# Dividing 544 tokens at 256 instead of at 272, with both parts of a result in one run of PSUM

## The chip, the cores and the metric

The kernel is one program on one core of one Trainium2 chip. TensorE multiplies, VectorE (DVE) and ScalarE (ACT) take the results out of PSUM, GpSimd (POOL) adds squares, and SyncE (SP) issues most transfers. The metric is the device time of one execution in microseconds.

## The reference

One decoder layer in float32 works on 512 prompt tokens and 8 x 4 sample tokens, 544 in all, each of 1024 values:

```
x = x + 0.5 * rmsnorm(swiglu(rmsnorm(x, f1_pre), f1_in, f1_out), f1_post)     # w_in 1024 x 5632, w_out 2816 x 1024
h = rmsnorm(x, mix_pre)
gq, gk, gv, gg, la, sq, sk, sv = project(h, w_in, gate_w, gate_b)             # 1024 x 3088
m = merge(gla(gq, gk, gv, la), gg, stick_breaking(sq, sk, sv, cache), w_out)  # 1024 x 1024
x = x + rmsnorm(m, mix_post)
x = x + 0.5 * rmsnorm(swiglu(rmsnorm(x, f2_pre), f2_in, f2_out), f2_post)
x = x + rmsnorm(sigmoid(rmsnorm(x, ple_pre) @ ple_w_gate) * (p @ ple_w_up), ple_post)
```

A dense product multiplies a weight matrix with the activations of all 544 tokens. The outputs are x and the new keys, values and states.

## The kernel before

Activations lie transposed: 128 features on the partitions, tokens along the row. `x`, `y`, `e`, `proj`, `rstd` and `glr` are declared with the tokens as two halves of `HALF = T // 2 = 272`, and `flat` (L106) joins the two to 544; the operands of the dense products, `a_hi`, `a_lo`, `h_hi` and `h_lo`, have plain rows of 544. Rows follow each other without gaps, so a row starts 2176 bytes after the one before.

A dense product is made of three products of type fp32r: each weight tile and each activation tile is split into a high part and the rest, and high x high, high x low and low x high are added up in PSUM. `dense` (L434) runs over the 128-row tiles `k` of the contraction, over one or two result tiles `c`, over the three combinations, and innermost over the two halves of the tokens. So each `mm` of L444 has a stationary operand of 128 x 128, which is loaded anew for each half, and a moving operand of 128 x 272. A PSUM bank holds 512 fp32 numbers per partition; half 0 of a result lies in columns 0 to 271 of one bank, half 1 in columns 0 to 271 of the next. Four banks are a quad; the steps of a stage use the two quads by turns. There are 8304 such products: 3168 in each of the two FFNs (`up0` 12 steps, `down0` 8, `up1` 10, `down1` 8), 1200 in the input projection `in` (its last step has 16 stationary columns), 384 in `out` and 384 in `gate`.

Other products over all tokens have the same division: the sums of squares (L455, `sum_norm`), the sums of the head norms (L807), the embedding (L490) and the gate logits (L639).

The readers of PSUM take both halves in one instruction, by `banks` (L280): a pattern of 2 x 272 numbers with a step of 512, or 4 x 272 for two result tiles. They are on DVE the gate and up parts of an FFN step (L1223, L1224), the second half of a down product (L1239), the projections (L1276, L1281, L1285), the forget gate (L1366), the first embedding (L1564) and the output gate (L1576); on ACT they are the norms (L859, L1097) and copies (L911, L1106, L1131).

The order of the work is written out by hand. Each engine runs its own program and waits on semaphores: TensorE waits for a split weight (`split_lo`), for a free quad (`psum_free`) and at the start of a stage for each input tile (`a_lo_ready`, `h_lo_ready`); the readers wait for `psum_full`, the last product of a step. SP loads a weight (two transfers of 512 KB) when the split of the weight two before it is done.

Of the kernel before, what the change touches and what calls it, by code (L numbers as in the profile page):

```python
# [20 lines left out]
P = 128  # L21
# [6 lines left out]
HALF = T // 2  # L28
# [77 lines left out]
def flat(ap):  # L106

    return ap.rearrange("p a t -> p (a t)")


def build(nc, a, o):
# [13 lines left out]
    with ctx:  # L125
# [8 lines left out]

        x = sb("x", [P, KD, 2, HALF])
        y = sb("y", [P, KD, 2, HALF])
# [22 lines left out]
        rstd = sb("rstd", [P, 2, 2, HALF])  # L159
        work = sb("work", [P, 2, T])  # L160
        glr = sb("glr", [GLA_RANK, 2, HALF])
# [18 lines left out]
        with nc.sbuf_tensor("proj", [P, 24, 2, HALF], F32) as proj:  # L180
            pass
        with nc.sbuf_tensor("rows", [P, 5, D_MODEL], F32) as rows, nc.sbuf_tensor("e", [P, KD, 2, HALF], F32) as e:
            pass
# [15 lines left out]
        gs = scratch(work_flat, 0, [P, 2, HALF])  # L199
        us = scratch(work_flat, T, [P, 2, HALF])  # L200
        dead = proj[:, SV:SV + 8].rearrange("p k a t -> p (k a t)")
# [7 lines left out]
        y_flat = y[:].rearrange("p k a t -> p (k a t)")  # L209
# [8 lines left out]
        q_pad = [rstd[:, n].rearrange("p a t -> p (a t)") for n in range(2)]  # L218
# [23 lines left out]
        la_raw, la_soft = rstd[:, 0].rearrange("p a t -> p (a t)"), sum_sq[:]  # L242
# [37 lines left out]
        def banks(quad, first, n):  # L280
            return PS[:, 4 * quad + first:4 * quad + first + n, 0:HALF]
# [139 lines left out]
        def _(pe):  # L421
# [58 lines left out]
            def embed(s_):  # L480

                t, slot = embed_ticket(s_), W0["embed"] % 2
                weights(W0["embed"])
                open_t(t)
                for k in range(2):
                    for c in range(2):
                        for n, (wt, act) in enumerate(((w_hi, p_hi), (w_hi, p_lo), (w_lo, p_hi))):
                            for half in range(2):
                                col = k * D_MODEL + (2 * s_ + c) * P
                                last = mm(PS[:, 4 * (t % 2) + 2 * c + half, 0:HALF], wt[:, slot, col:col + P],  # L490
                                          act[:, k, half * HALF:(half + 1) * HALF],
                                          start=(k == 0 and n == 0), stop=(k == 1 and n == 2))
                last.then_inc(sig["psum_full"], 1)
# [142 lines left out]
            def gate_logits(p):  # L636

                for half in range(2):
                    last = mm(PS[:, 6 + half, 0:HALF], gate_w[:, p * P:(p + 1) * P], glr[:, half], start=True, stop=True)  # L639
                last.then_inc(sig["la_full"], 1)  # L640
# [161 lines left out]
            for i in range(KD):  # L802
                t = T0["merge"] + i
                open_t(t)
                pe.wait_ge(sig["m_sq"], i + 1)
                for half in range(2):
                    last = mm(PS[:, 4 * (t % 2) + half, 0:HALF], (ones if i < 4 else ones64)[:],  # L807
                              sq[:, i % 2, half * HALF:(half + 1) * HALF], start=True, stop=True)
                last.then_inc(sig["psum_full"], 1)
# [32 lines left out]
        def _(act):  # L842
# [12 lines left out]
            def norm(j):  # L855

                t, r = sum_ticket[j], rstd[:, j % 2]
                full(act, t)
                fn(r, banks(t % 2, 0, 2), ACT.Ln, bias=eps[:], scale=1.0 / D_MODEL).then_inc(psum_free[t % 2], 1)  # L859
                act.wait_ge(psum_free[t % 2], t // 2 + 1)  # L860
                fn(r, r, ACT.Exp, scale=-0.5).then_inc(sig["rstd_ready"], 1)
# [47 lines left out]
            def down0(st, t, quad, use):  # L909
                full(act, t)  # L910
                fn(y[:, bass.ds(st.n, 1)].rearrange("p k a t -> p (k a) t"), banks(quad, 0, 2),  # L911
                   ACT.Copy).then_inc(psum_free[quad], 1)

            def down1(j):
                def body(st, t, quad, use):

                    act.wait_ge(psum_free[quad], use + 1)
                    n = 8 * j + st.n
                    act.wait_ge(sig["sq_used"], n - 1)
                    fn(sq[:, st.parity(0), :], y[:, bass.ds(st.n, 1)].rearrange("p k a t -> p (k a t)"),  # L920
                       ACT.Square).then_inc(sig["sq_ready"], 1)
                return body
# [167 lines left out]
            for i in range(KD):  # L1090
                if i + 1 < KD:
                    head_square(i + 1)
                t, r = T0["merge"] + i, rstd[:, i % 2]
                full(act, t)
                if i >= 2:
                    act.wait_ge(sig["m_ready"], i - 1)
                fn(r, banks(t % 2, 0, 2), ACT.Ln, bias=eps[:],  # L1097
                   scale=1.0 / (GLA_DV if i < 4 else SB_DH)).then_inc(psum_free[t % 2], 1)
                act.wait_ge(psum_free[t % 2], t // 2 + 1)
                fn(r, r, ACT.Exp, scale=-0.5).then_inc(sig["m_norm"], 1)  # L1100
                act.wait_ge(sig["m_ready"], i + 1)
                fn(a_hi[:, i, :], decay[i % 2], ACT.Copy).then_inc(sig["a_hi_ready"], 1)

            def out_body(st, t, quad, use):
                full(act, t)
                fn(y[:, 2 * st.c:2 * st.c + 2].rearrange("p k a t -> p (k a) t"), banks(quad, 0, 4),  # L1106
# [21 lines left out]
            def e_tiles(n):  # L1128
                t = embed_ticket(n)
                full(act, t)  # L1130
                fn(e[:, 2 * n:2 * n + 2].rearrange("p k a t -> p (k a) t"), banks(t % 2, 0, 4),  # L1131
# [30 lines left out]
        def _(dve):  # L1162
# [52 lines left out]
            def up(name, j):  # L1215
                base = up_base[name]

                def body(st, t, quad, use):
# [4 lines left out]
                    v.tensor_tensor(gs, banks(quad, 0, 2), r, ALU.mult).then_inc(sig["g_ready"], 1)  # L1223
                    v.tensor_tensor(us, banks(quad, 2, 2), r, ALU.mult).then_inc(psum_free[quad], 1)  # L1224
# [11 lines left out]
            def down1(st, t, quad, use):  # L1236
                full(dve, t)
                yt = y[:, bass.ds(st.n, 1)].rearrange("p k a t -> p (k a) t")
                v.tensor_tensor(yt, banks(quad, 0, 2), yt, ALU.add).then_inc(psum_free[quad], 1)  # L1239
# [33 lines left out]
            def project(st, t, quad, use):  # L1273
                full(dve, t)
                if st.c == 12:
                    v.tensor_tensor(glr[:], PS[0:GLA_RANK, 4 * quad:4 * quad + 2, 0:HALF], rstd[0:GLA_RANK, 0],  # L1276
                                    ALU.mult).then_inc(psum_free[quad], 1)
                elif st.c == 0:

                    for c in range(2):  # L1280
                        ins = v.scalar_tensor_tensor(proj[:, GQ + c], banks(quad, 2 * c, 2), GLA_DK ** -0.5,  # L1281
                                                     rstd[:, 0], ALU.mult, ALU.mult)
# [80 lines left out]
            for p in range(2):  # L1363
                dve.wait_ge(sig["la_full"], p + 1)
                dve.wait_ge(sig["cum_ready"], p)
                v.tensor_scalar(rstd[:, 0], PS[:, 6:8, 0:HALF], vec[:, 64 + p:65 + p], None,  # L1366
# [13 lines left out]
            for hh in range(2):  # L1380
                r = slice(64 * hh, 64 * hh + 64)
                dst = y[r, 4:8].rearrange("p k a t -> p k (a t)")[:, :, SEQ:T].rearrange("p k (b t) -> p k b t", t=DEC_SEQ)
# [116 lines left out]
            def sample_outs(p):  # L1499
                dve.wait_ge(sig["on_full"], p + 1)  # L1500
                src = PS[:, 4, 0:64].rearrange("p (b h t) -> p h b t", h=2, t=DEC_SEQ)
                dst = y[:, 2 * p:2 * p + 2].rearrange("p k a t -> p k (a t)")[:, :, SEQ:T].rearrange(
# [61 lines left out]
            v.tensor_copy(e[:, 0:2].rearrange("p k a t -> p (k a) t"), banks(t % 2, 0, 4)).then_inc(psum_free[t % 2], 1)  # L1564
            boundary(2, 5, "f2_post", "ple_pre", 4)
            for n in range(4):
# [8 lines left out]
                for c in range(2):  # L1575
                    ins = v.tensor_tensor(work[:, c, :].rearrange("p (a t) -> p a t", a=2), banks(quad, 2 * c, 2),  # L1576
# [9 lines left out]
        def _(pool):  # L1586
# [92 lines left out]
            for hh in range(2):  # L1679
                r = slice(64 * hh, 64 * hh + 64)  # L1680
                q_ = proj[r, SQ:SQ + 4].rearrange("p k a t -> p k (a t)")[:, :, SEQ:T].rearrange(
# [89 lines left out]
```

## Time and profile before

| | |
|---|---|
| time, median of 3 executions | 1465.97 us (1462.32 to 1467.61) |
| profiled execution, first to last instruction | 1466.9 us |
| TensorE (PE) busy | 1342.8 us, 92%, 9669 products |
| DVE busy | 607.3 us, 41% |
| ACT busy | 429.2 us, 29% |
| POOL busy | 147.9 us, 10% |
| DMA | 110.00 MB, mean 75 GB/s |

The profiled execution has no time of its own beside its span of 1466.9 us, which lies between the median and the highest of the three. Engines: PE is TensorE's products, PEld its weight loads, which run beside them. "L444" is line 444 of the kernel. A product's mean ns in the profile is its latency, from its first column in to its last out; products overlap, so the pace has to be read from the starts of neighbours. The clock column is the granted share of TensorE's 2.4 GHz. Times in the timeline are us from the start of the span, and one row of it may hold several instructions ("x2").

### The profile page before, as it was taken

What the parts mean: (1) busy time and instruction counts of PE and PEld (TensorE: products, weight loads), DVE (VectorE), ACT (ScalarE), POOL (GpSimd) and SP (SyncE); (2) the same over time, 40 slices, a digit from 0 to 9 for tenths busy, and PEclk for the clock granted to TensorE, in tenths of its full rate; (3) what the DMA queues carried; (4) which work ended last, traced back from release to release, by engine and by line L of the source; (5) the groups of instructions that cost most, each with busy time, mean ns of one, the idle gap of its engine ahead of it and who ended that gap; (6) DMA issues with size and microseconds to landing.
All of it is one profiled execution on the core that took longest, in us unless ns stands there. A gap on an engine that the chain in (4) does not pass through costs nothing.

```text
span 1466.9 us, 22802 instructions
## 1 busy us (share of the span) xinstructions
PE 1342.8 (92%) x9669; PEld 1271.9 (87%) x9669; DVE 607.3 (41%) x650; ACT 429.2 (29%) x497; POOL 147.9 (10%) x159
## 2 busy tenths in 40 slices
PE   3999999999995999989988878779999999999895
PEld 2999999999995999867777647779999999999894
DVE  5244422344337233234427743364443134433843
ACT  3222222222324111245411134432222222222543
POOL 3200000000013000010003301230000000001311
PEclk9999999999998999979956868889999999999997
DMA  6133233332231222311310002312322333223101
GB/s 174 32 86 86 75 87 99 99 92 73 72 107 44 86 86 59 134 43 43 130 44 17 15 17 73 87 30 72 93 78 75 99 99 86 75 73 102 67 29 61
DMA packets 168149, 110.00 MB, mean 75 GB/s; under 512 B 5147, under 2 KB 160878, under 8 KB 168094
## 3 DMA queue, kind: packets, MB, share of 16 engines
q1 hardware_dynamic: 166450, 104.15, 24.2%
q0 software_dynamic: 1472, 5.01, 1.1%
q8 instruction: 41, 0.67, 0.2%
q14 instruction: 14, 0.11, 0.0%
q10 hardware_dynamic: 172, 0.05, 0.0%
HBM read 103.57 MB, written 5.64 MB: 74 GB/s over the span
## 4 chain that ended last, share of the span: by engine, by line
PE 84%; DVE 9%; ACT 3%; issue 2%; SPq 1%; POOL 1%; DMA 0%; POOLq 0%; ACTq 0%; DVEq 0%
PE PS L444 70%; DVE work L1185 2%; PE PS L666 2%; DVE a_lo L1176 2%; PE PS L714 1%; DVE x L1197 1%; PE PS L577 1%; PE PS L606 1%; PE PS L772 1%; PE PS L455 1%; PE PS L775 1%; PE PS L603 1%; PE PS L586 1%; PE PS L555 1%; DMA raw<-in_f_in 0%
## 5 line engine op out<-in xcount | busy, mean ns | idle before, releaser
L444 PE MATMUL PS<-a_hi,w_hi 128*128 128x272 f32 (+1 forms) x2064 | 435.8, 293 | 39.6 <-DVE a_lo L1176 23.5
L444 PE MATMUL PS<-a_lo,w_hi 128*128 128x272 f32 (+1 forms) x2064 | 431.4, 291 | 0.0
L444 PE MATMUL PS<-a_hi,w_lo 128*128 128x272 f32 (+1 forms) x2064 | 430.6, 291 | 0.0
L444 PEld LDWEIGHTS PS<-a_hi,w_hi 128*128 128x128 f32 (+1 forms) x2064 | 327.5, 191 | 46.3 <-issue 21.9
L444 PEld LDWEIGHTS PS<-a_lo,w_hi 128*128 128x128 f32 (+1 forms) x2064 | 328.3, 191 | 0.5
L444 PEld LDWEIGHTS PS<-a_hi,w_lo 128*128 128x128 f32 (+1 forms) x2064 | 326.0, 191 | 0.5
L1170 DVE TENSOR_TENSOR w_lo<-raw,w_hi 128x2048 fp32r<-128x2048 f32 (+2 forms) x97 | 202.1, 2083 | 230.5 <-ACT w_hi L853 230.5
L853 ACT ACTIVATE w_hi<-raw 128x2048 fp32r<-128x2048 f32 (+2 forms) x97 | 166.0, 1712 | 116.2 <-PE PS L444 114.6
L444 PE MATMUL PS<-h_hi,w_hi 128*128 128x272 f32 x704 | 145.3, 287 | 0.0
L444 PE MATMUL PS<-h_hi,w_lo 128*128 128x272 f32 x704 | 144.8, 288 | 0.0
L444 PE MATMUL PS<-h_lo,w_hi 128*128 128x272 f32 x704 | 144.6, 287 | 0.0
L903 ACT ACTIVATE work<-work 128x544 f32<-128x544 f32 x44 | 29.0, 660 | 346.4 <-DVE work L1223 346.4
L1223 DVE TENSOR_TENSOR work<-PS,rstd 128x544 f32<-128x544 f32 x44 | 31.9, 725 | 237.2 <-PE PS L444 219.5
L444 PEld LDWEIGHTS PS<-h_lo,w_hi 128*128 128x128 f32 x704 | 110.0, 188 | 0.0
L444 PEld LDWEIGHTS PS<-h_hi,w_lo 128*128 128x128 f32 x704 | 109.6, 188 | 0.0
L444 PEld LDWEIGHTS PS<-h_hi,w_hi 128*128 128x128 f32 x704 | 109.6, 188 | 0.0
L1623 POOL TENSOR_TENSOR sum_sq<-sum_sq,sq 128x544 f32<-128x544 f32 x56 | 87.5, 1562 | 180.0 <-ACT sq L868 91.1
L1620 POOL COPY sum_sq<-sq 128x544 f32<-128x544 f32 x8 | 5.1, 638 | 729.9 <-ACT sq L920 677.2
L1285 DVE TENSOR_TENSOR proj<-PS,rstd 128x1088 f32 (+1 forms) x11 | 14.2, 1292 | 91.3 <-PE PS L444 91.3
L1231 DVE TENSOR_TENSOR h_lo<-work,h_hi 128x544 f32 (+1 forms) x44 | 31.9, 726 | 40.3 <-ACT h_hi L905 40.3
L1176 DVE SCALAR_TENSOR_TENSOR a_lo<-x,vec,a_hi 128x544 fp32r<-128x544 f32 x32 | 39.8, 1243 | 3.7 <-ACT a_hi L873 3.2
L911 ACT ACTIVATE y<-PS 128x544 f32 (+1 forms) x16 | 10.0, 626 | 105.9 <-PE PS L444 105.9
(299 smaller groups left out, 1164.8 us busy)
## 6 DMA issues: line engine op xcount, KB each, us to landing
raw<-in_f_in SPq DMA_DIRECT2D x88, 512.0 KB, 5.0
raw<-in_f_out SPq DMA_DIRECT2D x32, 384.0 KB, 4.0
raw<-in_w_in SPq DMA_DIRECT2D x24, 512.0 KB, 4.6
raw<-in_f_out SPq DMA_DIRECT2D x32, 320.0 KB, 3.6
raw<-in_w_out SPq DMA_DIRECT2D x8, 512.0 KB, 4.4
y<-in_cache_sb_k SPq DMA_DIRECT2D x16, 256.0 KB, 2.6
raw<-in_ple_w_gate SPq DMA_DIRECT2D x8, 512.0 KB, 3.9
rows<-in_x_prompt SPq DMA_DIRECT2D x4, 512.0 KB, 4.9
```

The lines of the kernel that those rows point to most:

```text
L444: last = mm(PS[0:width, 4 * quad + 2 * c + half, 0:HALF], wt[:, slot, cols], act[:, k, half * HALF:(half + 1) * HALF], start=(k == 0 and n ...
L455: last = mm(PS[:, 4 * (t % 2) + half, 0:HALF], ones[:], sum_sq[:, half * HALF:(half + 1) * HALF], start=True, stop=True)
L555: mm(PS[:, 0, j * P:(j + 1) * P], k_[:, j * P:(j + 1) * P], q_[:, j * P:(j + 1) * P], start=True, stop=True)
L666: last = mm(PS[:, 2 + p, b * 8:b * 8 + 8], v_page[j][:, p * P:(p + 1) * P], w_past[:, pg * 256 + col:pg * 256 + col + 8], start=False, sto ...
L853: fn(w_hi[:, slot, 0:width], raw[:, slot, 0:width], ACT.Copy).then_inc(sig["split_hi"], 1)
L903: fn(gs, gs, ACT.Silu).then_inc(sig["silu_ready"], 1)
L1170: v.tensor_tensor(w_lo[:, slot, 0:width], raw[:, slot, 0:width], w_hi[:, slot, 0:width].bitcast(F32), ALU.subtract).then_inc(sig["split_lo ...
L1176: v.scalar_tensor_tensor(a_lo[:, k, :], flat(x[:, k]), vec[:, c:c + 1], a_hi[:, k, :].bitcast(F32), ALU.mult, ALU.subtract).then_inc(sig[" ...
L1185: v.scalar_tensor_tensor(work[:, k % 2, :], flat(y[:, k]), vec[:, c:c + 1], flat(rstd[:, j % 2]), ALU.mult, ALU.mult).then_inc(sig["upd_re ...
L1223: v.tensor_tensor(gs, banks(quad, 0, 2), r, ALU.mult).then_inc(sig["g_ready"], 1)
L1231: v.tensor_tensor(h_lo[:, hs, :].rearrange("p a t -> p (a t)"), flat(us), h_hi[:, hs, :].bitcast(F32).rearrange("p a t -> p (a t)"), ALU.s ...
L1623: g.tensor_tensor(sum_sq[:], sum_sq[:], sq[:, k % 2, :], ALU.add).then_inc(sig["sq_used"], 1)
```

## The change

The tokens are divided into 256 and 288. `x`, `y`, `e`, `proj`, `rstd`, `glr`, and the scratch tiles `gs` and `us`, become plain rows of 544 at the same size and the same place, and `flat` returns its argument. Part 0 of a result goes to columns 256 to 511 of its first bank, part 1 to columns 0 to 287 of the next, so the 544 numbers lie without a gap across the border of the two banks. Products, banks, quads, semaphores, waits and transfers are the same in number and order.

```
+SPLIT_AT = 256
+HALVES = (slice(0, SPLIT_AT), slice(SPLIT_AT, T))
...
-    return ap.rearrange("p a t -> p (a t)")
+    return ap
...
-        def banks(quad, first, n):
-            return PS[:, 4 * quad + first:4 * quad + first + n, 0:HALF]
+        PSF = PS[:].rearrange("p b n -> p (b n)")
+        def half_out(bank, half, rows_=slice(0, P)):
+            return PS[rows_, bank, 512 - SPLIT_AT:512] if half == 0 else PS[rows_, bank + 1, 0:T - SPLIT_AT]
+        def tokens(bank, rows_=slice(0, P)):
+            return PSF[rows_, bank * 512 + 512 - SPLIT_AT:bank * 512 + 512 - SPLIT_AT + T]
+        def token_pair(quad):
+            return PSF[:, quad * 2048:quad * 2048 + 2048].rearrange("p (c n) -> p c n", c=2)[
+                :, :, 512 - SPLIT_AT:512 - SPLIT_AT + T]
...
-                                last = mm(PS[0:width, 4 * quad + 2 * c + half, 0:HALF], wt[:, slot, cols],
-                                          act[:, k, half * HALF:(half + 1) * HALF],
+                                last = mm(half_out(4 * quad + 2 * c, half, slice(0, width)), wt[:, slot, cols],
+                                          act[:, k, HALVES[half]],
...
-                    last = mm(PS[:, 4 * (t % 2) + half, 0:HALF], ones[:], sum_sq[:, half * HALF:(half + 1) * HALF],
+                    last = mm(half_out(4 * (t % 2), half), ones[:], sum_sq[:, HALVES[half]],
...
-                fn(y[:, bass.ds(st.n, 1)].rearrange("p k a t -> p (k a) t"), banks(quad, 0, 2),
+                fn(y[:, bass.ds(st.n, 1)].rearrange("p k t -> p (k t)"), tokens(4 * quad),
...
-                    v.tensor_tensor(gs, banks(quad, 0, 2), r, ALU.mult).then_inc(sig["g_ready"], 1)
-                    v.tensor_tensor(us, banks(quad, 2, 2), r, ALU.mult).then_inc(psum_free[quad], 1)
+                    v.tensor_tensor(gs, tokens(4 * quad), r, ALU.mult).then_inc(sig["g_ready"], 1)
+                    v.tensor_tensor(us, tokens(4 * quad + 2), r, ALU.mult).then_inc(psum_free[quad], 1)
...
-                                    banks(quad, 0, 4).rearrange("p (c a) t -> p c a t", c=2),
-                                    rstd[:, 0:1].broadcast_to([P, 2, 2, HALF]), ALU.mult).then_inc(psum_free[quad], 1)
+                                    token_pair(quad),
+                                    rstd[:, 0:1].broadcast_to([P, 2, T]), ALU.mult).then_inc(psum_free[quad], 1)
```

The remaining products (L490, L639, L807) and readers are changed in the same way.

## Rows read from the trace of the kernel before

**Rows 1.** The page, part 4: the chain that ended last, its shares by line.

```profile
PE PS L444 70%; DVE work L1185 2%; PE PS L666 2%; DVE a_lo L1176 2%; PE PS L714 1%; DVE x L1197 1%; PE PS L577 1%; PE PS L606 1%; PE PS L772 1%; PE PS L455 1%; PE PS L775 1%; PE PS L603 1%; PE PS L586 1%; PE PS L555 1%; DMA raw<-in_f_in 0%
```

**Rows 2.** Busy time by stretch: us, then each engine's busy us and (instructions).

```profile
core 0: us, PE busy (x) PEld busy (x) DVE busy (x) ACT busy (x) POOL busy (x), PEclk, DMA share, GB/s
...
53.40:438.60 385.20, 385.20 (x3072) 384.98 (x3072) 140.17 (x130) 98.12 (x97) 8.82 (x7) 1.00 0.30 85
...
473.40:613.00 139.60, 139.59 (x1104) 138.18 (x1105) 39.62 (x23) 24.45 (x14) 0.00 (x0) 0.99 0.27 84
...
978.40:1368.00 389.60, 389.41 (x3100) 388.71 (x3100) 141.86 (x132) 100.73 (x100) 10.19 (x8) 1.00 0.30 87
...
1399.70:1438.70 39.00, 38.98 (x288) 38.80 (x288) 11.71 (x12) 11.08 (x14) 7.45 (x6) 0.92 0.06 21
```

**Rows 3.** Groups by form: names, shapes, count, busy us, mean ns, idle before.

```profile
L444 PE MATMUL PS<-a_hi,w_hi 128*128 128x272 f32 x2048 | 432.5, 293 | 39.6 <-DVE a_lo L1176 23.5 <-DVE work L1224 5.8 <-issue 4.4
...
L444 PE MATMUL PS<-h_hi,w_hi 128*128 128x272 f32 x704 | 145.3, 287 | 0.0
...
L444 PE MATMUL PS<-a_hi,w_hi 128*16 128x272 f32 x16 | 3.3, 288 | 0.0
```

**Rows 4.** Timeline of PE, split products at full clock: start us, us, form, count.

```profile
249.73 0.41 PE L444 MATMUL PS<-h_hi,w_hi 128*128 128x272 f32 x2
...
255.70 0.41 PE L444 MATMUL PS<-h_hi,w_hi 128*128 128x272 f32 x2
```

**Rows 5.** Timeline of PE, products with 16 stationary columns.

```profile
607.06 0.41 PE L444 MATMUL PS<-a_hi,w_hi 128*16 128x272 f32 x2
...
612.79 0.41 PE L444 MATMUL PS<-a_hi,w_lo 128*16 128x272 f32 x2
```

**Rows 6.** Timeline of PE, half clock and its end.

```profile
979.41 0.66 PE L444 MATMUL PS<-a_hi,w_hi 128*128 128x272 f32 x2
...
982.13 0.61 PE L444 MATMUL PS<-a_hi,w_hi 128*128 128x272 f32 x2
982.58 0.41 PE L444 MATMUL PS<-a_lo,w_hi 128*128 128x272 f32 x2
982.83 0.41 PE L444 MATMUL PS<-a_hi,w_lo 128*128 128x272 f32 x2
```

**Rows 7.** Timeline of PE, plain fp32 products of 384, 256 and 128 columns.

```profile
654.07 0.81 PE L591 MATMUL PS<-extra,tri 128*128 128x384 f32 x2
654.72 0.59 PE L592 MATMUL PS<-extra,ones 128*128 128x256 f32 x2
655.15 0.38 PE L593 MATMUL PS<-extra,ones 128*128 128x128 f32 x2
655.37 0.39 PE L594 MATMUL PS<-extra,ones 128*128 128x128 f32 x2
```

**Rows 8.** Timeline of PEld, weight loads for products of 8 columns; the group they belong to.

```profile
658.43 1.86 PEld L577 LDWEIGHTS PS<-sq,work 128*128 128x128 f32 x16 [0.17 <-issue]
...
L577 PEld LDWEIGHTS PS<-sq,work 128*128 128x128 f32 x128 | 14.9, 191 | 2.1 <-issue 1.2 <-ACT work L979 0.9
```

**Rows 9.** Groups by form: readers of PSUM on DVE and ACT.

```profile
L1223 DVE TENSOR_TENSOR work<-PS,rstd 128x544 f32<-128x544 f32 x44 | 31.9, 725 | 237.2 <-PE PS L444 219.5 <-ACT rstd L861 17.7
...
L1285 DVE TENSOR_TENSOR proj<-PS,rstd 128x1088 f32 x10 | 12.9, 1292 | 80.9 <-PE PS L444 80.9
...
L911 ACT ACTIVATE y<-PS 128x544 f32 x12 | 7.5, 626 | 83.7 <-PE PS L444 83.7
...
L1319 DVE TENSOR_TENSOR extra<-proj,PS 128x512 f32<-128x512 f32 x8 | 5.5, 688 | 15.9 <-PE PS L594 15.9
...
L1157 ACT ACTIVATE rows<-PS 128x512 f32<-128x512 f32 x8 | 4.8, 598 | 7.3 <-PE PS L834 7.3
...
L1106 ACT ACTIVATE y<-PS 128x1088 f32<-128x1088 f32 x4 | 4.3, 1079 | 31.5 <-PE PS L444 31.5
```

**Rows 10.** The chain in order of time: start us, us, what.

```profile
53.35 385.26 PE PS L444 x3072
```

More of the change, by code:

```diff
@@ L179, in build @@
             pass
-        with nc.sbuf_tensor("proj", [P, 24, 2, HALF], F32) as proj:
+        with nc.sbuf_tensor("proj", [P, 24, T], F32) as proj:
             pass
-        with nc.sbuf_tensor("rows", [P, 5, D_MODEL], F32) as rows, nc.sbuf_tensor("e", [P, KD, 2, HALF], F32) as e:
+        with nc.sbuf_tensor("rows", [P, 5, D_MODEL], F32) as rows, nc.sbuf_tensor("e", [P, KD, T], F32) as e:
             pass
@@ L198, in build @@
         work_flat = work[:].rearrange("p a t -> p (a t)")
-        gs = scratch(work_flat, 0, [P, 2, HALF])
-        us = scratch(work_flat, T, [P, 2, HALF])
-        dead = proj[:, SV:SV + 8].rearrange("p k a t -> p (k a t)")
+        gs = scratch(work_flat, 0, [P, T])
+        us = scratch(work_flat, T, [P, T])
+        dead = proj[:, SV:SV + 8].rearrange("p k t -> p (k t)")
         extra_flat = extra[:]
@@ L216, in build @@
         k_turned = scratch(work_flat, 0, [P, 2, 512])
-        q_pad = [rstd[:, n].rearrange("p a t -> p (a t)") for n in range(2)]
+        q_pad = [rstd[:, n] for n in range(2)]
         q_block = scratch(sq_flat, 0, [P, 4, DEC_BATCH, 8])
@@ L489, in embed @@
                                 col = k * D_MODEL + (2 * s_ + c) * P
-                                last = mm(PS[:, 4 * (t % 2) + 2 * c + half, 0:HALF], wt[:, slot, col:col + P],
-                                          act[:, k, half * HALF:(half + 1) * HALF],
+                                last = mm(half_out(4 * (t % 2) + 2 * c, half), wt[:, slot, col:col + P],
+                                          act[:, k, HALVES[half]],
                                           start=(k == 0 and n == 0), stop=(k == 1 and n == 2))
@@ L638, in gate_logits @@
                 for half in range(2):
-                    last = mm(PS[:, 6 + half, 0:HALF], gate_w[:, p * P:(p + 1) * P], glr[:, half], start=True, stop=True)
+                    last = mm(half_out(6, half), gate_w[:, p * P:(p + 1) * P], glr[:, HALVES[half]], start=True, stop=True)
                 last.then_inc(sig["la_full"], 1)
@@ L806, in _ @@
                 for half in range(2):
-                    last = mm(PS[:, 4 * (t % 2) + half, 0:HALF], (ones if i < 4 else ones64)[:],
-                              sq[:, i % 2, half * HALF:(half + 1) * HALF], start=True, stop=True)
+                    last = mm(half_out(4 * (t % 2), half), (ones if i < 4 else ones64)[:],
+                              sq[:, i % 2, HALVES[half]], start=True, stop=True)
                 last.then_inc(sig["psum_full"], 1)
@@ L858, in norm @@
                 full(act, t)
-                fn(r, banks(t % 2, 0, 2), ACT.Ln, bias=eps[:], scale=1.0 / D_MODEL).then_inc(psum_free[t % 2], 1)
+                fn(r, tokens(4 * (t % 2)), ACT.Ln, bias=eps[:], scale=1.0 / D_MODEL).then_inc(psum_free[t % 2], 1)
                 act.wait_ge(psum_free[t % 2], t // 2 + 1)
@@ L1096, in _ @@
                     act.wait_ge(sig["m_ready"], i - 1)
-                fn(r, banks(t % 2, 0, 2), ACT.Ln, bias=eps[:],
+                fn(r, tokens(4 * (t % 2)), ACT.Ln, bias=eps[:],
                    scale=1.0 / (GLA_DV if i < 4 else SB_DH)).then_inc(psum_free[t % 2], 1)
@@ L1105, in out_body @@
                 full(act, t)
-                fn(y[:, 2 * st.c:2 * st.c + 2].rearrange("p k a t -> p (k a) t"), banks(quad, 0, 4),
+                fn(y[:, 2 * st.c:2 * st.c + 2], token_pair(quad),
                    ACT.Copy).then_inc(psum_free[quad], 1)
@@ L1130, in e_tiles @@
                 full(act, t)
-                fn(e[:, 2 * n:2 * n + 2].rearrange("p k a t -> p (k a) t"), banks(t % 2, 0, 4),
+                fn(e[:, 2 * n:2 * n + 2], token_pair(t % 2),
                    ACT.Copy).then_inc(psum_free[t % 2], 1)
@@ L1237, in down1 @@
                 full(dve, t)
-                yt = y[:, bass.ds(st.n, 1)].rearrange("p k a t -> p (k a) t")
-                v.tensor_tensor(yt, banks(quad, 0, 2), yt, ALU.add).then_inc(psum_free[quad], 1)
+                yt = y[:, bass.ds(st.n, 1)].rearrange("p k t -> p (k t)")
+                v.tensor_tensor(yt, tokens(4 * quad), yt, ALU.add).then_inc(psum_free[quad], 1)
             def ffn(name, j):
@@ L1280, in project @@
                     for c in range(2):
-                        ins = v.scalar_tensor_tensor(proj[:, GQ + c], banks(quad, 2 * c, 2), GLA_DK ** -0.5,
+                        ins = v.scalar_tensor_tensor(proj[:, GQ + c], tokens(4 * quad + 2 * c), GLA_DK ** -0.5,
                                                      rstd[:, 0], ALU.mult, ALU.mult)
@@ L1563, in _ @@
             full(dve, t)
[L1564 removed]
+            v.tensor_copy(e[:, 0:2], token_pair(t % 2)).then_inc(psum_free[t % 2], 1)
             boundary(2, 5, "f2_post", "ple_pre", 4)
@@ L1575, in _ @@
                 for c in range(2):
-                    ins = v.tensor_tensor(work[:, c, :].rearrange("p (a t) -> p a t", a=2), banks(quad, 2 * c, 2),
+                    ins = v.tensor_tensor(work[:, c, :], tokens(4 * quad + 2 * c),
                                           rstd[:, 0], ALU.mult).then_inc(psum_free[quad] if c else sig["pg_ready"], 1)
@@ L1680, in _ @@
                 r = slice(64 * hh, 64 * hh + 64)
-                q_ = proj[r, SQ:SQ + 4].rearrange("p k a t -> p k (a t)")[:, :, SEQ:T].rearrange(
+                q_ = proj[r, SQ:SQ + 4][:, :, SEQ:T].rearrange(
                     "p k (b t) -> p k b t", t=DEC_SEQ)
```

23 lines of the change are left out of this document (11 added, 12 removed).

## The prediction

> **What bounds the kernel now.** I read the chain first. 70% of the span is L444, the fp32r products of the dense stages [rows 1]; the next line has 2%. In time order an FFN is one piece of it, 385.26 us with 3072 products and no break [rows 10]. The table by stretch says the same from the other side: in the FFNs, the input projection and the gate TensorE is busy for the whole stretch, while DVE is busy for 140.17 and ACT for 98.12 of 385.20 us, and DMA for 0.30 [rows 2]. The groups then say how many products there are: three combinations with 2048, 704 and 16 each, 8304, or 4152 pairs of halves [rows 3]. Their mean of 293 or 287 ns is a latency and no pace.
>
> So the time hangs on the pace of one product of 272 columns. At full clock it comes from the starts of two rows: 249.73 and 255.70 are 24 pairs apart, 5.97 / 48 = 124.4 ns for a product [rows 4]. With tile changes in it, it is 385.20 / 3072 = 125.4 ns [rows 2]. I take 125. The dense products are 8304 x 125 = 1038 us of the 1466.9.
>
> **What sets 125 ns.** Three groups narrow it down.
> - At half clock 12 products take 982.13 - 979.41 = 2.72 us, 226.7 ns each [rows 6], exactly 272 columns at 1.2 GHz. At 2.4 GHz the same columns are 113.3 ns. So at full clock 125 - 113.3 = 11.7 ns are something else, which half clock hides entirely.
> - It is not the loading of weights. With 16 stationary columns in place of 128, 607.06 to 612.79 is 23 pairs, 5.73 / 46 = 124.6 ns [rows 5]. And 16 loads of 128 columns for products of only 8 columns take 1.86 us, with the last one's own 0.19 in it: (1.86 - 0.19) / 15 = 111 ns [rows 8].
> - It is not general to products. Plain fp32 products, whose records use two cycles a column (384 columns 0.325 us, 256 columns 0.215, 128 columns 0.11 [rows 7]), follow 2N / 2.4 + about 3 ns.
> - An instruction stream that is late looks unlikely. After 12 and more products at 227 ns, in which a stream that needs 125 would have run ahead, the first pair at full clock already takes 982.83 - 982.58 = 0.25 us [rows 6].
>
> What is left is the path of the moving operand or of the result at one column per cycle: either about 11.7 ns for each product, or a rate of 272 / 125 = 2.18 columns per ns in place of 2.4. The trace has fp32r products of 272 columns and of no other width, so it can't tell these apart.
>
> **Part 1: the halves become 256 and 288.** Nothing is removed or added; each pair still has 544 columns and two products.
> - As a cost for each product: 106.7 + 11.7 = 118.4 and 120 + 11.7 = 131.7, sum 250.1 ns, against 2 x 125 = 250.
> - As a rate: 256 / 2.18 = 117.4 and 288 / 2.18 = 132.1, sum 249.5.
> - As a fixed beat of 125 for any product, with 288 columns still inside it (120 plus the 3 ns of rows 7): 250.
>
> All three give 0 us. The shorter product must still cover the next weight load: 117.4 is above 111 [rows 8], so it does, by 6 ns. The bounds: if the short product's 256 columns went at the pace of plain fp32 (106.7 + 3 = 109.7, held up at 111) and the long one stayed at 125, a pair would lose 14 ns, 4152 x 14 = 58 us; if the short one stayed at 125 and the long one took 132.1, it would gain 7.1 ns, 29.5 us. I take 0, as the value to which two linear laws and the beat all lead, and keep both ends. The position of the operand in its row changes too (half 1 starts at byte 1024 and no longer at 1088); of this no row has a price, and 0.25 us stands for every pair in rows 4 to 6 whatever its tile. I allow 1 ns a product either way, 8 us.
>
> The Trainium skill (TensorE: Matmul & The Clock Gate, Back-to-back issue gap) gives an isolated product N / 2.4 + 2.5 ns, 115.8 at 272. The trace has 124.4 [rows 4], so the rule misses this kernel's products by 9 ns, and agrees with rows 7. By it a pair would be 231.7 ns at either division, also a change of 0.
>
> **Part 2: the other products over tokens** (L455, L490, L639, L807). The fp32 ones are linear in the columns [rows 7], so 256 + 288 costs what 272 + 272 did: 0. The embedding's 96 are of the kind of part 1.
>
> **Part 3: the readers of PSUM take one run.** A DVE reading of PSUM in one run of 512 takes 688 ns, one in two runs of 272 takes 725, and 1088 in four takes 1292 [rows 9]. The slope is (1292 - 725) / 544 = 1.04 ns a number, and 688 + 32 x 1.04 = 721. So the gap in the pattern costs at most 4 ns of 725. On ACT the slope is (1079 - 626) / 544 = 0.83, and 598 + 32 x 0.83 = 625 against 626: nothing. The 44 + 44 + 16 + 11 readings in the dense stages lie beside TensorE, which is busy all the time; DVE could be 245 us longer there before it mattered [rows 2]. On the path stand only those at stage borders, some 25 (norms, first FFN step, output gate): 25 x 4 = 0.1 us at most. That a run crosses a bank border could cost instead of give; a copy of 512 in one bank and 1088 over two pairs of banks show nothing that depends on it. I take 0, with +-0.1.
>
> **Part 4: plain rows in SBUF.** The addresses of `x`, `y`, `proj` stay, and every SBUF reader already got 544 numbers in a run by `flat`. No wait, semaphore or transfer is added or moved. 0.
>
> **Sum.** 0 + 0 + 0 + 0 against the profiled execution of 1466.9 us, which is 0.9 above the median of the three; I forecast 1466 us.
>
> **Rivals.**
> - *A: the operand comes in blocks.* If the moving operand is fetched in whole blocks of 32 columns, 272 counts as 9 blocks, 125 / 9 = 13.9 ns each, and half clock (26.7 ns a block's time) hides all but the array's own. Then 256 is 8 blocks, 111 ns, just at the weight load, and 288 is 9, 125. A pair drops from 250 to 236, and the dense stages by 4152 x 14 = 58 us, less the few at half clock: 1410 us. If the block is of 64 columns and starts at fixed addresses, rows of 2176 bytes put every second `k` in the middle of a block: there 256 columns touch 5 blocks as before, and the gain is half, 29 us: 1438 us. For it: 11.7 ns unexplained beside two evenly cut parts, and 288 / 2.4 = 120 is most of 125. Against: the two halves of 272 start at different places in a block, and no pair in rows 4 to 6 is shorter; plain fp32 records are fully linear.
> - *B: the longer part costs more and the shorter gives nothing back.* If a successor can't start before a beat of 125 and a product over 272 columns pays its 132, a pair takes 257. It decides from the point where a 256-column product still holds its successor for 125 ns. 4152 x 7 = 29 us: 1495 us, slower than before. For it: the pace did not move when the stationary operand shrank [rows 5], as a beat would have it. Against: products and loads at 109 to 111 ns exist [rows 7, 8], and beat and rate would both have to meet at 272.
> - *C: alignment alone.* The law is linear, but half 1's new start saves or costs 1 ns or more a product: 1458 or 1474 us, and a bit beyond.
>
> On A: the Trainium skill (SBUF — State Buffer, Door 1: The DMA port swizzle) gives SBUF lines of 16 bytes. 1088, 1024 and 1152 bytes are all whole lines, so by it nothing is rounded, and A's gain would be 0. No row here shows the line.
>
> **How the numbers follow.** What a measurement of this kernel can tell from no change is about 0.5%, 7.3 us: 1458.6 to 1473.3. Forecast (linear or beat): 0.45, nearly all of it within that band, own range 1459 to 1473. A: 0.27 (blocks of 32 and 64 about equal). B: 0.12. C beyond the band: 0.16, evenly. So faster 0.27 + 0.08 = 0.35, slower 0.12 + 0.08 = 0.20, same 0.45. The range goes down to A's far end, with which it reaches 1409, and up to 1477, over C but short of B; left out are B and the tails, about 0.17.
>
> **What would show it.** Starts of L444 pairs at full clock still 0.25 us apart, with about 0.118 us from part 0 to part 1 and 0.132 from part 1 to the next. 0.236 for a pair is A; 0.257, with 0.125 for the first step, is B. L1223 at 721 to 725 ns and L911 at 625 confirm part 3; over 740 would refute it. Half clock must show 0.213 and 0.240 us under every theory. The forecast is wrong if the 3072 products of the FFN stretches take less than 381 or more than 389 us.

## The result, and the profile after

The changed kernel takes 1473.35 us (median, 1467.80 to 1474.44), the kernel before 1466.79 us beside it (1462.32 to 1469.42): the ratio is 1.0049, with a 95% interval of 1.0033 to 1.0066. That is 6.6 us more. The profiled execution took 1474.09 us, with a span of 1472.4 us; that of before had 1466.9 us.

The chain of waits still runs through the same pieces. L457 is what was L444. First the changed kernel (start us, us, what):

```profile
34.77 15.05 PE PS L457 x96
53.62 388.06 PE PS L457 x3072
...
444.67 2.17 PE PS L468 x4
...
477.47 140.66 PE PS L457 x1104
894.81 49.66 PE PS L457 x384
982.09 388.07 PE PS L457 x3072
1406.14 38.01 PE PS L457 x288
```

and the pieces of the kernel before that [rows 10] doesn't have:

```profile
34.66 14.89 PE PS L444 x96
...
441.61 1.17 PE PS L455 x4
...
473.40 139.80 PE PS L444 x1104
891.82 48.99 PE PS L444 x384
978.44 385.28 PE PS L444 x3072
1399.72 39.01 PE PS L444 x288
```

The pieces of dense products grow by 0.16 + 2.80 + 0.86 + 0.67 + 2.79 - 1.00 = 6.3 us. The last term is the gate, where full clock was granted sooner: the stretches of after show 0.96 there, against 0.92 in [rows 2]. Outside the dense products the two largest differences come with the granted clock: four products of L468 take 2.17 us at a clock of 0.50 instead of 1.17 at 1.00, and the attention part is 1.9 us shorter, with a mean clock of 0.79 against 0.76. All in all it is 5.5 us between the two spans. So nothing but the dense products has become slower at the same clock, each by a little, and without a break in the chain.

In the dense stages nothing else moved. The stretches (us, then each engine's busy us and instructions, clock, DMA share, GB/s) show it:

```profile
53.60:441.70 388.10, 388.04 (x3072) 387.82 (x3072) 140.15 (x131) 98.12 (x97) 8.82 (x7) 1.00 0.30 84
...
1406.10:1444.10 38.00, 37.95 (x288) 37.81 (x288) 11.71 (x12) 11.10 (x14) 7.44 (x6) 0.96 0.06 21
```

DVE's 140.15, ACT's 98.12, POOL's 8.82 and the DMA share of 0.30 are those of [rows 2]; the granted clock is 1.00 in both.

The pace at full clock, in the timeline of PE over the same products as [rows 4]. One row holds the two parts of a pair:

```profile
249.89 0.41 PE L457 MATMUL PS<-h_hi,w_hi 128*128 128x256 f32 x2
250.14 0.41 PE L457 MATMUL PS<-h_lo,w_hi 128*128 128x256 f32 x2
250.38 0.41 PE L457 MATMUL PS<-h_hi,w_lo 128*128 128x256 f32 x2
...
255.92 0.41 PE L457 MATMUL PS<-h_hi,w_hi 128*128 128x256 f32 x2
```

24 pairs from 249.89 to 255.92 are 6.03 / 48 = 125.6 ns a product, where [rows 4] gave 124.4. Over all distances between starts of neighbours at full clock the mean was 124.88 ns and is 125.76 (distances of 160 ns and more, which are waits, are left out; below, "pace" is this mean). 8304 x 0.88 ns = 7.3 us: that is the loss. Within a pair the 256 columns hold their successor for 118.3 ns on average, the 288 columns for 133.3.

At half clock a pair costs what it must (timeline of the first FFN's begin):

```profile
35.36 0.66 PE L457 MATMUL PS<-a_lo,w_hi 128*128 128x256 f32 x2
...
40.35 0.65 PE L457 MATMUL PS<-a_hi,w_hi 128*128 128x256 f32 x2
```

11 pairs in 4.99 us are 453.6 ns each; 544 columns at 1.2 GHz are 453.3, and the kernel before had 2 x 226.7 [rows 6]. The single distances are 213.3 and 240.4 ns on average. The loss exists at full clock only.

The readers of PSUM, which now see one run of 544 or two of 544 (groups by form):

```profile
L1236 DVE TENSOR_TENSOR work<-PS,rstd 128x544 f32<-128x544 f32 x44 | 31.9, 725 | 240.8 <-PE PS L457 222.9 <-ACT rstd L874 17.9
...
L1298 DVE TENSOR_TENSOR proj<-PS,rstd 128x1088 f32 x10 | 12.9, 1292 | 81.6 <-PE PS L457 81.6
...
L924 ACT ACTIVATE y<-PS 128x544 f32 x12 | 7.5, 625 | 84.7 <-PE PS L457 84.7
```

725, 1292 and 625 ns, against 725, 1292 and 626 in [rows 9]. The gap in the pattern had cost nothing, and a run across the border of two banks costs nothing in these readings.

### The profile page after: what moved, and what is told of

Its sections match the earlier page's. It is cut to its first block, busy times and chain, and to the rows that moved or that the text cites. A ratio compares the mean times of both kernels' runs of the same rounds, so it can differ in the third digit from the quotient of the medians.

```text
span 1472.4 us, 22802 instructions
## 1 busy us (share of the span) xinstructions
PE 1346.6 (91%) x9669; PEld 1276.7 (87%) x9669; DVE 607.2 (41%) x650; ACT 428.9 (29%) x497; POOL 148.3 (10%) x159
## 4 chain that ended last, share of the span: by engine, by line
PE 86%; DVE 7%; ACT 3%; issue 1%; SPq 1%; POOL 1%; DMA 0%; POOLq 0%; ACTq 0%; DVEq 0%
PE PS L457 71%; PE PS L727 2%; PE PS L679 2%; DVE work L1198 1%; DVE a_lo L1189 1%; PE PS L590 1%; DVE x L1210 1%; PE PS L619 1%; PE PS L468 1%; PE PS L503 1%; PE PS L785 1%; PE PS L616 1%; PE PS L599 1%; PE PS L568 1%; PE PS L756 1%
## 5 line engine op out<-in xcount | busy, mean ns | idle before, releaser
L457 PE MATMUL PS<-a_hi,w_hi 128*128 128x256 f32 (+2 forms) x2064 | 437.8, 294 | 39.9 <-DVE a_lo L1189 22.4
L457 PE MATMUL PS<-a_hi,w_lo 128*128 128x256 f32 (+2 forms) x2064 | 432.7, 291 | 0.0
L457 PE MATMUL PS<-a_lo,w_hi 128*128 128x256 f32 (+2 forms) x2064 | 431.2, 290 | 0.0
L457 PEld LDWEIGHTS PS<-a_hi,w_hi 128*128 128x128 f32 (+1 forms) x2064 | 337.1, 191 | 46.8 <-issue 23.8
L457 PEld LDWEIGHTS PS<-a_lo,w_hi 128*128 128x128 f32 (+1 forms) x2064 | 338.1, 191 | 0.5
L457 PEld LDWEIGHTS PS<-a_hi,w_lo 128*128 128x128 f32 (+1 forms) x2064 | 334.6, 190 | 0.5
L457 PE MATMUL PS<-h_hi,w_lo 128*128 128x256 f32 x704 | 146.1, 288 | 0.0
L457 PE MATMUL PS<-h_lo,w_hi 128*128 128x256 f32 x704 | 145.5, 288 | 0.0
L457 PE MATMUL PS<-h_hi,w_hi 128*128 128x256 f32 x704 | 145.2, 288 | 0.0
L457 PEld LDWEIGHTS PS<-h_hi,w_hi 128*128 128x128 f32 x704 | 113.8, 189 | 0.0
L457 PEld LDWEIGHTS PS<-h_lo,w_hi 128*128 128x128 f32 x704 | 113.5, 189 | 0.0
L457 PEld LDWEIGHTS PS<-h_hi,w_lo 128*128 128x128 f32 x704 | 112.8, 188 | 0.0
L1298 DVE TENSOR_TENSOR proj<-PS,rstd 128x1088 f32 (+1 forms) x11 | 14.2, 1292 | 92.1 <-PE PS L457 92.1
```

The costliest lines, as they stand in the source:

```text
L457: last = mm(half_out(4 * quad + 2 * c, half, slice(0, width)), wt[:, slot, cols], act[:, k, HALVES[half]], start=(k == 0 and n == 0), stop ...
```

## The experiments

The operands' places used below are worked out from the declarations: `a_hi`, `a_lo`, `h_hi` and `h_lo` start 96 bytes behind a multiple of 256 in their partition, `w_hi` and `w_lo` 128 bytes behind one (each tile is taken as rounded up to 32 bytes, and the first as starting 128 bytes behind a multiple of 256; another first start would shift all of them alike, and the loops too). Rows of activations are 2176 bytes apart, 17 x 128. "Base" is such a remainder. A run of a whole layer is read by its pace and its ratio to the kernel before; a table at the end of this section has them all.

### widths: the law of one product, alone

The rest of the layer is left out, here and in the two other loops below.

```
for i in range(48):  # one group; other groups change columns, starts and type
    mm(PS[0:128, i % 2, 0:N], w[:, i % 16 * 128:i % 16 * 128 + 128], act[:, start:start + N], start=True, stop=True)
```

> Not the layer, but 48 groups of 48 fp32r or bf16 products in a row on TensorE, each group with one width, one start of the moving operand in its row, one width of the stationary operand; the rest of the computation is left out. Theory 1, a rate with an effect of position: at full clock a product of N fp32r columns takes about 0.46 N ns from start to start (256: 118, 272: 125, 288: 132, 512: 236) and starts at 0, 32, 64, 96 ... bytes differ by 1 to 4 ns; with 16 stationary columns the effect of position is gone; bf16 at 272 takes 116. Rival 2, a cost for each product: N / 2.4 + 11.7 ns (256: 118, 288: 132, 512: 225). Rival 3, the layout in PSUM is what costs: then all starts in a row give the same time, since every result here begins at the first column of a bank.

The chain has one row for each group of 48 products: L75 is 224 columns, L77 240, L79 256, L81 272, L83 288, L87 384, L89 448, L91 512; L95 is 256 columns with the moving operand 64 bytes on, L97 96 bytes on; L153 is bf16 with 512 columns.

```profile
58.70 5.37 PE PS L75 x48
64.07 5.37 PE PS L77 x48
69.44 5.75 PE PS L79 x48
75.19 6.02 PE PS L81 x48
81.21 6.33 PE PS L83 x48
...
94.57 8.32 PE PS L87 x48
102.89 9.91 PE PS L89 x48
112.81 10.93 PE PS L91 x48
...
129.34 5.44 PE PS L95 x48
134.78 5.75 PE PS L97 x48
...
298.10 10.36 PE PS L153 x48
```

A 48th of a row is the pace: 111.9 twice, then 119.8, 125.4, 131.9, 173.3, 206.5 and 227.7 ns up to 512 columns. What is over N / 2.4 is 13.1 ns at 256 columns, 12.1 at 272, 11.9 at 288, 13.3 at 384, 19.8 at 448 and 14.4 at 512. Neither of the prediction's laws is met: at 512 the cost for each product (225.0) is near and the rate (235.3) is not, at 448 the rate (205.9) is near and the cost (198.4) is not. But neither the beat nor the block is there either: 256, 272 and 288 columns lie about 6 ns apart, so rivals A and B fall. 224 columns take no less than 240: there is a floor of about 112 ns. The weight loads of [rows 8] have 111; that they set the floor is likely but not tested.

The new thing is the start: the same 256 columns take 119.8 ns from byte 0, 113.3 ns from byte 64 (L95) and 119.8 from byte 96 (L97), 6.5 ns for nothing but the place. That refutes the rival of the PSUM layout, since every result here begins at the first column of a bank. For 288 columns all starts lie between 131.7 and 133.3 ns, for 272 columns between 123.5 and 126.7. With 16 stationary columns and 256 moving ones it was 116.7 ns from byte 0 and 113.5 from byte 96, so the effect of place is still there, although it had been expected to go. A 32-byte shift of the weights alone moved 119.8 to 118.3.

The Trainium skill (TensorE: Matmul & The Clock Gate, Back-to-back issue gap) gives N / 2.4 + 2.5 ns for an isolated product. The bf16 groups agree with it to 0.1 ns (55.8 at 128 columns once the group runs, 109.2 at 256, 215.8 at 512), the fp32r ones of 256 to 512 columns from byte 0 miss it by 9 to 17 ns.

### even_one_run: the new layout of PSUM, the old division

```
-SPLIT_AT = 256
+SPLIT_AT = 272
```

> The changed kernel with the division back at 272, still with both parts of a result in one run of PSUM and with plain rows. Theory 1, position of the moving operand and widths: a pair of products is at 250 ns again and the time that of the kernel before, ratio 1.000 +- 0.002. Rival 3, the PSUM layout or the readers across the bank border cost: it stays slower than before by 0.5%, about 1473 us.

The ratio is 1.0005 (0.9992 to 1.0019), the pace 124.87 ns. One run in PSUM, the readers' patterns and the plain rows cost nothing; the whole loss belongs to the division.

### moved_160 and moved_160_272: the activations lie 160 bytes further

```
+        gap = sb("gap", [P, 40])
         sum_sq = sb("sum_sq", [P, T])
```

in the changed kernel, and the same in the kernel before.

> The changed kernel with an unused tile of 160 bytes ahead of the sums of squares, so that the activation tiles begin 160 bytes further on (a multiple of 256 bytes in place of 96 over one); division at 256 as changed. Theory 1: the mean pace of a product moves by 0.5 to 2 ns from 125.8, that is the time by 4 to 16 us from 1473; I expect down, towards 124.5 and 1462. Rival (a product's time depends on its width alone): the mean stays at 125.8 and the ratio to before at 1.005.

> The kernel before (division at 272) with the same unused 160 bytes. Theory 1: its pace moves from 124.9 too, by 0.5 to 1.5 ns either way (4 to 12 us); rival, width alone: ratio 1.000 +- 0.002.

moved_160: ratio 1.0006 (0.9993 to 1.0019), pace 124.94, where 124.5 had been expected. moved_160_272: ratio 1.0053 (1.0036 to 1.0069), pace 125.47. Unused bytes turn the order around: with them the division at 256 costs nothing and the one at 272 costs 0.5%. So it is not the division as such that is slow, but the division at this place. The saving sits in the longer part: the 256 columns hold their successor for 118.2 ns (118.3 in the changed kernel), the 288 columns for 131.7 (133.3), and 4152 x 1.6 ns is 6.6 us.

### order_of_the_stage: the dense loop alone, at eight places

```
for k, c, n, half in order(tiles, 12):  # the order of dense; one or two result tiles
    mm(PS[0:128, 2 * c + half, 0:width], (w_hi, w_hi, w_lo)[n][...], (hi, lo, hi)[n][:, base + k * 544 + ...], ...)
```

> Not the layer, but 54 groups of fp32r products in the order of the kernel's dense loop (rows k of 2176 bytes, three combinations of high and low parts, two halves), 72 or 96 products each, with the division, the start of row 0 past a multiple of 256 bytes, and the width of the stationary operand as named; the rest of the computation is left out. Theory 1 (TensorE's own reading of the two operands sets the pace, and nothing else of the kernel takes part): mean ns a product for one result tile: division 272, base 96: 124.5; 272, base 0: 125.3; 256, base 96: 125.5; 256, base 0: 124.7, each within 0.2, as in the down stages of the four whole kernels; other bases and divisions between 122 and 127. With 16 stationary columns 124.5 at either division. Rival 4 (the other engines' and the transfers' traffic in SBUF takes part): without them the pace falls towards 116 or loses its dependence on base.

The chain has one row a group. One result tile, 72 products: L73 is the division at 256 from base 0, L79 from base 96; L89 and L95 the division at 272 from 0 and 96; L105 and L111 at 288. Two result tiles, 96 products: L173 and L175 are the division at 256 from 0 and 96, L177 and L179 at 272.

```profile
40.68 9.00 PE PS L73 x72
...
67.71 9.05 PE PS L79 x72
...
112.80 9.02 PE PS L89 x72
...
139.86 8.96 PE PS L95 x72
...
184.88 8.93 PE PS L105 x72
...
491.97 11.99 PE PS L173 x96
503.96 12.08 PE PS L175 x96
516.04 12.06 PE PS L177 x96
528.10 12.04 PE PS L179 x96
```

A row over its count has the change from the group before in it; the mean over 48 distances from the 13th product on (72 with two tiles) is sharper. Carried on to the end of the group it moves by up to 0.25 ns, so differences below that are not read. One tile, ns a product:

| base | 0 | 32 | 64 | 96 | 128 | 160 | 192 | 224 |
|---|---|---|---|---|---|---|---|---|
| 256 / 288 | 124.71 | 125.60 | 124.79 | 125.54 | 124.73 | 125.46 | 124.69 | 125.56 |
| 272 / 272 | 125.29 | 125.62 | 125.00 | 124.46 | 125.27 | 125.94 | 125.00 | 124.48 |
| 288 / 256 | 123.90 | 125.29 | 125.29 | 125.56 | 124.02 | 125.27 | 125.33 | 125.35 |

The `down` stages of whole kernels (one tile) have 124.46 (before, base 96), 125.55 (after, base 96), 124.72 (moved_160, base 0) and 125.28 (moved_160_272, base 0). The bare loop gives the same within 0.03 ns, without any other engine at work and without a transfer. Contention with other engines or transfers for SBUF is refuted; TensorE alone makes the difference. Base b and base b + 128 agree within 0.35 ns: rows `k` lie 17 x 128 bytes apart, so that each group sees both by turns. With two tiles bases 0 and 96 give 124.79 and 125.83 for 256, 125.47 and 125.21 for 272. The kernel before happens to stand where 272 is at its best, and 256 near its worst. The divisions at 240, 264 and 280, tried at the same eight bases, lie between 125.0 and 127.0.

With 16 stationary columns, base 96, the loop has 124.12 for 256 and 124.79 for 272 (124.5 had been expected for both): the loss is gone. The layer says the same. In the last step of its input projection, which has 16 stationary columns, the pace is 124.6 ns in both kernels, the two widths weighed alike.

### weights_and_pitch: is it the moving operand's place, or its place to the weights'?

The same loop; the weights start at other bytes too, and rows are 2176 or 2304 bytes apart.

> Not the layer, but 41 groups of fp32r products in the order of the dense loop as in the run before, with the start of the weight tile past a multiple of 256 bytes, the distance of two rows k (2176 or 2304 bytes) and the order of combinations and halves as named; the rest of the computation is left out. Theory 1a, only the place of the moving operand against a multiple of 256 bytes counts: shifting the weights changes the mean by less than 0.1 ns; with rows 2304 apart every row has its start, base 0 and base 128 give the same. Theory 1b, it is where the two reads of TensorE stand to each other: shifting the weights changes the mean by 0.3 to 1.5 ns too. Both: all means lie between 123 and 127 ns; two result tiles with division 288, base 0: 124.0 +- 0.4.

L96 to L104 are the division at 256 from base 0 with the weights at 0, 32, 64, 96 and 192 bytes; L106 to L114 are the same with base 96.

```profile
245.79 8.97 PE PS L118 x72
254.76 9.05 PE PS L120 x72
...
281.87 9.00 PE PS L126 x72
290.87 9.00 PE PS L128 x72
299.87 9.12 PE PS L130 x72
...
317.98 9.00 PE PS L134 x72
...
345.01 9.10 PE PS L140 x72
```

By the mean from the 13th product on, the 256 / 288 groups fall into two sets, 124.7 to 124.8 and 125.4 to 125.6, by the difference of the two starts modulo 128 (moving less stationary):

| difference | 0 | 32 | 64 | 96 |
|---|---|---|---|---|
| base 0 | 124.83 | 125.56 | 124.75, 124.79 | 125.54 |
| base 96 | 124.73 | 125.50, 125.60 | 124.79 | 125.38 |

In this division neither operand's place counts by itself: base 96, the slow one of the changed kernel, is fast as soon as the weights go to 96 or 32. That refutes theory 1a, which allowed 0.1 ns. Of ten groups with the divisions at 272 and 288, nine repeat within 0.25 ns the value that their difference had with the weights at 128; one doesn't (272, difference 64: 124.48 in place of 125.00; L118 above, beside L120 with 125.67). With rows of 2304 bytes, 9 x 256, the pace is 125.00, 125.00 and 126.67 ns for the division at 256 from base 0, 64 and 96 (L126, L128, L130), and 125.00 and 126.67 for 272 from base 0 and 128 (L134, L140). So the distance of the rows belongs to it: where the rows no longer alternate, 128 bytes can make a difference too (for 256 they don't, base 128 has 125.00 again). The shortest pace of all loops is there, 123.33 ns for 288 from base 64. The order counts as well: with each half's three products one after the other, in place of the two halves by turns, 288 / 256 from base 0 takes 125.50 ns and not 123.90.

### split_288 and split_288_moved: the longer part first

```
-SPLIT_AT = 256
+SPLIT_AT = 288
```

in the changed kernel, and with the 160 unused bytes as well.

> The changed kernel with the parts the other way round, 288 first and 256 behind, activations where they are (96 past a multiple of 256 bytes). By the group with that division and base, 125.56 ns against 124.46 of the kernel before, theory 1 expects 8304 x 0.9 = 7 us more than before, ratio 1.005. Rival, the harm is in a first part of 256 or in columns 256 to 511 of the bank: ratio 1.000.

> The same with the unused 160 bytes ahead, so that the activations begin at a multiple of 256 bytes. By its group, 123.90 ns, theory 1 expects 8304 x (-0.6 to -1.0) = 5 to 8 us less than the kernel before, ratio 0.9955 +- 0.0015, the best of the arrangements measured. Rival, width and position cancel in the whole kernel: ratio 1.000.

split_288: ratio 1.0018 (1.0004 to 1.0031), pace 125.16; split_288_moved: 0.9996 (0.9980 to 1.0012), pace 124.80. Both are misses in size. The one-tile `down` stages came out as in the bare loop (125.57 and 123.89 ns, against 125.56 and 123.90). But three quarters of the products (6144 of 8304) are in stages with two result tiles, and those had 125.0 and 125.1 to 125.2, not the one-tile values from which I had reckoned. The bare loop with two tiles, run with weights_and_pitch, has 125.00 and 124.79 for them, where I had expected 124.0 +- 0.4 for the second; against the layer it is 0.3 ns short there. So the gain in `down` is given back in the stages beside it: no version tried beats the kernel before by more than the noise.

### both_moved and weights_moved: the same question in the whole layer

```
         raw = sb("raw", [P, 2, SLOT])
+        gap_w = sb("gap_w", [P, 40])          # both_moved; 24 in weights_moved
...
+        gap = sb("gap", [P, 8])               # weights_moved only
         sum_sq = sb("sum_sq", [P, T])
```

> The changed kernel, whole, with 160 unused bytes a partition ahead of w_hi, so that the weights and all activations start 160 bytes later; everything is computed. Theory 'relative position' (only the place of the moving operand's start to the stationary operand's, modulo 128 bytes, counts): nothing changes in the pace, 125.76 ns a product, one-tile down stages 125.55, ratio about 1.005. Rival 'the activations' own place' (the row of h and a in a line of SBUF counts by itself, the weights' doesn't): as moved_160, 124.94 and 124.72 ns, ratio about 1.0006.

> The changed kernel, whole, with 96 unused bytes ahead of w_hi and 32 ahead of sum_sq: the weights start 96 bytes later, the activations 128 bytes later, which is their old place modulo 128. Everything is computed. Theory 'relative position': the difference of the starts is that of moved_160, so the pace is 124.94 ns a product, the down stages 124.72, the ratio about 1.0006. Rival 'the activations' own place': their place modulo 128 is unchanged, so 125.76 and 125.55 ns, ratio about 1.005.

First fence both_moved, second weights_moved, from their chains:

```profile
52.97 388.06 PE PS L458 x3072
...
980.51 388.06 PE PS L458 x3072
```

```profile
52.27 386.72 PE PS L459 x3072
...
975.78 385.01 PE PS L459 x3072
```

With both operands moved by 160 bytes the FFN takes 388.06 us, to a hundredth what the changed kernel takes, though its activations are now at base 0, where moved_160 was fast. With the weights moved against the activations, whose base modulo 128 is the old one, the loss is gone: the pace is 124.84 ns, the `down` stages have 124.7. (386.72 us is more than the 385.26 of before because this FFN began with 6.1 us at half clock, before's with 3.4.) For the division at 256 the relative place decides; the rival is out. In the whole layer the division at 272 was moved only together with the distance to the weights, so for it the same is shown by the loop alone, but for L118.

### All whole kernels

"Difference" is the moving operand's start less the stationary one's, modulo 128 bytes.

| kernel | division | difference | pace, ns | ratio | interval |
|---|---|---|---|---|---|
| before | 272 | 96 | 124.88 | 1 | |
| after | 256 | 96 | 125.76 | 1.0049 | 1.0033 to 1.0066 |
| even_one_run | 272 | 96 | 124.87 | 1.0005 | 0.9992 to 1.0019 |
| moved_160 | 256 | 0 | 124.94 | 1.0006 | 0.9993 to 1.0019 |
| moved_160_272 | 272 | 0 | 125.47 | 1.0053 | 1.0036 to 1.0069 |
| both_moved | 256 | 96 | 125.75 | 1.0049 | 1.0031 to 1.0067 |
| weights_moved | 256 | 0 | 124.84 | 1.0002 | 0.9990 to 1.0013 |
| split_288 | 288 | 96 | 125.16 | 1.0018 | 1.0004 to 1.0031 |
| split_288_moved | 288 | 0 | 124.80 | 0.9996 | 0.9980 to 1.0012 |

8304 x (pace - 124.88) / 1466 gives 1.0050, 0.9999, 1.0003, 1.0033, 1.0049, 0.9998, 1.0016 and 0.9995 for the rows after the first. All but one are inside their interval; for moved_160_272 the 1.0033 is just below the interval, which begins at 1.0036. The pace explains nearly all of every ratio.

## Why the prediction was right, and where it was not

The forecast was 1466 us and the time is 1473.35: inside the range (1409 to 1477), but just beyond the forecast's own band (1459 to 1473), and by the ratio, 1.0049, just within the 0.5% that the prediction takes as no change. The interval begins at 1.0033, so the kernel is really slower: the sum of nothings was not quite nothing. That the time lies in the range is owed to the allowance of 1 ns for the place, a guess that no row had borne out.

- **What bounds the kernel:** right. All of the difference lies in the dense products, at full clock, and 0.88 ns of pace times 8304 is 7.3 us. An FFN piece took 388.06 us, inside the 381 to 389 that the prediction had set as its limits.
- **Part 1, the law of the columns:** the width by itself costs nothing, as forecast, but the reason was only half right. The parts take 118.3 and 133.3 ns where 117.4 to 118.4 and 131.7 to 132.1 were worked out; with the operands at another distance (moved_160) they take 118.2 and 131.7, which is the cost for each product. The experiment on widths, up to 512 columns, agrees neither with that cost nor with the rate alone, and the beat, the third way to 0, does not exist.
- **Part 1, the place of the operand:** the term that was mis-sized. The prediction had it at 0 with 1 ns either way, because pairs of 272 columns at two places both took 0.25 us. It came to +0.88 ns, 7.3 of the 8 us allowed. Those pairs were no evidence: a row of the timeline rounds to 10 ns, and a pair sums two starts, which hides just the effect in question. The prediction also looked at half 1's new start alone, whereas what counts is the place of both halves to the weights'.
- **Part 2:** no sign against it. The four products of L468 that took 1.00 us longer ran at half clock; in the piece before the first FFN they take 0.93 us in both kernels.
- **Part 3:** confirmed by 725, 1292 and 625 ns, and by even_one_run as a whole.
- **Part 4:** confirmed by even_one_run, which has the plain rows and keeps the old pace.
- **Rival A, blocks:** refuted. 256 columns in the layer take 118.3 ns and not 111. The effect by place has something of a block in it (113.3 ns for 256 columns from byte 64), but no pair of 544 columns in any loop is shorter than 246.7 ns (2 x 123.33), where A has 236.
- **Rival B, the beat:** refuted, 125 ns is no floor: 256 columns release their successor after 118.3.
- **Rival C, alignment alone:** this is what happened, at 1473.4 where its slow side had 1474. It had a chance of 0.16 beyond the band; the likeliest case took in the rest of it.

On the places: the Trainium skill (SBUF — State Buffer, Door 1: The DMA port swizzle) gives lines of 16 bytes. Every start here is a whole number of such lines, and a step of 32 bytes changed the pace of the loop by up to 1.4 ns (288 / 256, base 0 to 32: 123.90 to 125.29) all the same. That rule does not foresee it.

## What to carry to other kernels

Where back-to-back products set the time, a change of a product's width also changes where each operand starts, and for the fp32r products of this kernel that alone is worth 0.5%; before such a change is judged, run it once more with some unused bytes ahead of one operand. Do the same to the version that wins, since a tuned kernel may stand on a lucky place, as this one does. A row of the timeline is too coarse for 1 ns a product: take the length of a long unbroken piece of the chain over its count.

## What the runs showed of the hardware that was not expected

- An fp32r product of 128 stationary columns has a floor of about 112 ns (224 and 240 columns). From 256 columns on it takes 12 to 20 ns more than N / 2.4 when it starts at byte 0, and as little as 6.7 from byte 64 (256 columns); bf16 takes 2.5 ns more. Why fp32r costs more is not shown.
- The pace hangs on the starts of the moving and the stationary operand to each other. In the loop with rows 2176 bytes apart their difference modulo 128 bytes accounts within 0.25 ns for 19 of the 20 groups with moved weights. With 16 stationary columns the loss of the changed kernel is gone. That the two reads of TensorE meet in some way would fit both, but the mechanism itself was not seen.
- Stages with two result tiles have a second pace that the place does not set. At difference 0 with the division at 256 an `up` stage has either 124.7 or 125.3 ns a product, in every one of its steps of 96 products at full clock and never in between: in weights_moved the second stage of the first FFN has 125.27 and the same stage of the second FFN 124.72, in moved_160 both stages of the first FFN and the second of the second have 125.27 and the one left has 124.72. That is worth 0.5 to 0.6 us a stage. What picks the pace stays open. In before, after and both_moved all these stages have one pace (125.0, 125.8 and 125.8), and the two FFNs agree within 0.02 us.
- A whole FFN is no sharp measure of it, since the granted clock at its start differs too. In weights_moved the two FFNs take 386.72 and 385.01 us, and most of the difference is clock: the first begins with 6.1 us at 0.50, the second has a mean of 0.59 over its first 4.1 us, 3.4 of them at half clock (the stretches below).

```profile
52.27:58.37 6.10, 6.10 (x27) 6.10 (x28) 3.67 (x3) 2.98 (x3) 0.00 (x0) 0.50 0.00 0
975.78:979.90 4.12, 4.12 (x21) 4.12 (x22) 1.69 (x3) 2.99 (x3) 0.00 (x0) 0.59 0.00 0
```
